# Output projection inside the merges' block, first gather in the cross attention, value weights inside paged attention

## The chip, the cores and the metric

The kernel runs on one core of a Trainium2 chip. The metric is the device time of one execution in microseconds (us); of several executions the median is given. TensorE is PE in the rows (PEld is its weight load), VectorE is DVE, ScalarE ACT, GpSimd POOL, and SP the engine that issues most transfers (SPq its queue).

## The reference, cut to what matters

One layer of a decoder for 1024 prompt tokens and 64 new tokens (8 requests of 8). All branches read the same normalised input `h`.

```
z = h @ w_in, cut into queries, latents, gates, values ...
o_a: prompt: causal attention; new tokens: attention over 4096 cached
     positions per request, whose latent and rotary rows lie in pages
     (cache_kv_latent[page_table], cache_k_rope[page_table])
o_b: gated linear recurrence; its values are one block of 512 columns of z
o_c: attention into 256 memory tokens (memory keys and values per request)
proj = einsum('btne,ned->btnd', [o_a*silu, o_b*silu, o_c*silu], w_branch)
gate = sigmoid(g_raw)                      # three gates of 1024 channels
y = einsum('btd,de->bte', sum_n(gate * proj), w_out)
out = rmsnorm(x + y) * g_final
```

## The kernel before, in words

The program is a row of blocks. In a block each engine has a stream of its own, and the streams meet by semaphores; between blocks all engines meet. Tokens are 1088 columns (1024 prompt, 64 new); `h` and the merged result lie transposed, as 8 chunks of 128 channels.

Products of the projections are made of **split operands**: x is cut into a high part (a mask that clears the low bits, VectorE, `masked`, L884) and a low part (x less the high part, VectorE or GpSimd), ScalarE copies the high part into the rounded type (CAST), and TensorE adds three products: high by high, low by high, high by low. So each weight is loaded, masked, subtracted and copied before its first product.

The blocks that matter here, in order of time:

- **Cross attention** (block L1043, 683.6 to 762.2 us). SP loads the memory keys and values of four requests first (L1048, L1050), four more later. GpSimd only clears `qx` (L1099). TensorE turns the keys (L1198, waits for each request's keys) between the prompt's scores (L1167), turns (L1175) and products (L1184).
- **Paged attention** (block L1337, to 1025.5 us). The 8 requests go in 4 pairs; a pair has one step with the new tokens and 8 steps with a group of cached rows, so STEPS is 36. A group is four indirect transfers by GpSimd (latent rows L1376, rotary rows L1379, for two requests; 1.18 MB in all) into one of 8 slots; a slot is free when its group has been attended (`s_pv`). GpSimd also makes the pair's operands: a copy of the latent queries `qb` (L1363) and the rotary queries spread over quadrants `qpx` (L1365). In step k TensorE does the scores of k (L1530, L1533 for new tokens, L1542, L1546 for groups), turns the probabilities of k-1 (L1557, L1560), turns the rows of group k+1 (L1514, L1519) and attends k-1 (L1570, L1576). VectorE has the maximum of step k (L1424, L1426 or L1428), evacuates the probabilities (L1483, L1485) and half of the turned rows (L1490), keeps sums and accumulates (L1454). ScalarE has the exponentials (L1400, L1403) and the other half (L1411, L1413). SP loads the mask of the new tokens (L1341) and `w_uv` (L1342), after step 9 spills the gated branches to DRAM (L1344, L1345), brings `h`'s high part back (L1349), and spills the new tokens' branch (L1351) as soon as VectorE has gated it. The block ends when that spill has landed. Then the semaphores are cleared (L1609), with an empty block behind.
- **Value projection** (block L1664, to 1090.3 us). SP loads the value weights in four pieces (L1668), then constants. VectorE masks each piece and subtracts pieces 0 and 2 (L1713), GpSimd 1 and 3 (L1690), ScalarE copies (L1697); TensorE goes chunk by chunk over 8 token tiles in 8 banks (L1745).
- **Recurrence**, which the change leaves as it is.
- **Merges** (block L2414, 1495 to 1913.8 us): 48 items, 24 for each half of the tokens; item k is a channel block and a branch. An item is a gate product (48 matmuls, L2623, except two per half) and a branch product (24, L2648) of 272 columns. Its weights are loaded into one of three slots by SP (L2428, L2429) when `s_bp` says that the slot's last item is projected, masked by VectorE three items ahead (`prepare`, L884), subtracted by GpSimd (L2533), copied by ScalarE (L2572). ScalarE makes the sigmoid (L2584), VectorE the product with it (`consume`, L2499), GpSimd adds to the merged result (L2544).
- **Output projection** (block L2706). `w_out` is 4.2 MB, loaded as four pieces (L2713), split as above (VectorE L884, L2778; GpSimd L2805; ScalarE L2740), 8 chunks of 1024 columns. A tile of 128 tokens has its own split (L2770, L2800, L2736) and 48 matmuls of 512 columns (L2822); nine tiles alternate between two pairs of banks. VectorE adds the residual (L2789), ScalarE sums squares and takes the root, VectorE scales (L2763), SP stores (L2711).

The order within each stream is the order of the program text.

## Time and profile before

| what | us |
|---|---|
| median of 3 executions (lowest, highest) | 2040.85 (2038.68, 2044.95) |
| the profiled execution | 2041.31 |
| its span in the profile | 2039.5 |
| mean granted TensorE clock in it | 0.967 of full |

All times in rows are us from the span's start, of this one execution; 1.8 us of its time lie outside the span. In a timeline row the bracket is the idle time of the engine before the instruction and what ended it. Matmuls overlap, so their durations are longer than their spacing. PEclk is the granted clock as a share of full speed, DMA the mean busy share of 16 DMA engines.

### The profile page before, as it was taken

Reading aid. Unit: us, or ns where it says so; the run is one execution under the profiler, and the core shown is the slowest. Engines: PE = TensorE matmul, PEld = TensorE weight load, DVE = VectorE, ACT = ScalarE, POOL = GpSimd, SP = SyncE. Lnnn points to the kernel's source line nnn. Section 1 sums busy time; section 2 is a strip of 40 time slices with the busy share of each in tenths; the row PEclk is TensorE's granted clock in tenths of the full one; section 3 lists DMA queues with packets and bytes.
Section 4 is the critical chain, followed back from the end, with each engine's and each line's share of the span. In section 5 each row is a group of like instructions: output and inputs, shape, how many; then the busy total and the mean of one; then the engine's idle time right before and its main releaser. Section 6 shows DMA issues by size and latency. Waiting matters only on the chain. (4 is left out here: it accounts for less than half of the span.)

```text
span 2039.5 us, 31621 instructions
## 1 busy us (share of the span) xinstructions
PE 1872.0 (92%) x13519; PEld 1521.7 (75%) x13519; DVE 776.7 (38%) x1495; ACT 596.5 (29%) x1160; POOL 510.5 (25%) x392
## 2 busy tenths in 40 slices
PE   5998889887999878999978999999999999999798
PEld 4643455555999635666657989989889999999676
DVE  4025355556000243444421555465552115111432
ACT  3020333334111332323202343433332223222221
POOL 0000000004221007655006700000015454445320
PEclk8998999988999998999989999999999999999899
DMA  8002000001211317865022822222133334333322
GB/s 280 0 0 71 6 11 6 6 1 60 91 42 42 121 47 230 305 218 175 1 78 69 218 63 51 61 51 51 43 113 83 94 82 131 91 94 81 127 73 83
DMA packets 188519, 175.96 MB, mean 86 GB/s; under 512 B 47676, under 2 KB 155772, under 8 KB 188252
## 3 DMA queue, kind: packets, MB, share of 16 engines
q1 hardware_dynamic: 165228, 120.76, 20.2%
q0 software_dynamic: 20592, 52.63, 8.6%
q8 instruction: 107, 1.75, 0.4%
q10 hardware_dynamic: 2560, 0.56, 0.2%
q14 instruction: 32, 0.26, 0.0%
HBM read 153.73 MB, written 27.47 MB: 89 GB/s over the span
## 5 line engine op out<-in xcount | busy, mean ns | idle before, releaser
L884 DVE TENSOR_SCALAR sb<-sb 128x1024 int32<-128x1024 int32 (+4 forms) x127 | 97.8, 777 | 318.9 <-DMA sb<-in_w_branch 160.2
L2533 POOL TENSOR_TENSOR weights_low<-sb 128x1536 fp32r<-128x1536 f32 x42 | 147.1, 3501 | 183.7 <-DVE sb L884 183.7
L2623 PE MATMUL ps<-h_high_again,weights_high 128*128 128x272 f32 x688 | 142.2, 288 | 2.0 <-ACT weights_high L2572 2.0
L2623 PE MATMUL ps<-h_low,weights_high 128*128 128x272 f32 x688 | 142.3, 288 | 0.0
L2623 PE MATMUL ps<-h_high_again,weights_low 128*128 128x272 f32 x688 | 142.2, 288 | 0.0
L615 POOL TENSOR_TENSOR sb<-sb 32x1088 f32<-32x1088 f32 x8 | 19.9, 2483 | 394.1 <-ACT sb L626 394.1
L2160 PE MATMUL ps<-h_high_again,recurrence_weights_high 128*128 128x384 f32 (+1 forms) x432 | 105.4, 353 | 5.4 <-ACT recurrence_weights_high L1918 4.1
L2623 PEld LDWEIGHTS ps<-h_high_again,weights_high 128*128 128x128 f32 x688 | 108.2, 188 | 2.2 <-ACT weights_high L2572 2.2
L2623 PEld LDWEIGHTS ps<-h_high_again,weights_low 128*128 128x128 f32 x688 | 108.4, 188 | 0.0
L2623 PEld LDWEIGHTS ps<-h_low,weights_high 128*128 128x128 f32 x688 | 108.3, 188 | 0.0
L2572 ACT CAST weights_high<-sb 128x1536 fp32r<-128x1536 f32 (+1 forms) x44 | 64.3, 1461 | 130.6 <-POOL weights_low L2533 127.2
L2160 PE MATMUL ps<-h_high_again,recurrence_weights_low 128*128 128x384 f32 (+1 forms) x432 | 97.0, 334 | 0.0
L2160 PE MATMUL ps<-h_low,recurrence_weights_high 128*128 128x384 f32 (+1 forms) x432 | 96.8, 333 | 0.0
L975 PE MATMUL ps<-h_high,gate_weights_high 128*128 128x384 f32 (+1 forms) x384 | 85.5, 331 | 12.1 <-ACT h_high L950 10.8
L454 PE MATMUL ps<-sb 128*128 128x384 f32 (+3 forms) x288 | 89.8, 475 | 3.2 <-DMA sb<-in_w_in 3.2
L1376 POOL DMA_INDIRECT sb<-in_cache_kv_latent,sb x64 | 60.7, 948 | 119.2 <-issue 93.9
L2499 DVE TENSOR_TENSOR sb<-ps,sb 128x544 f32<-128x544 f32 x48 | 34.8, 724 | 137.1 <-PE ps L2648 132.1
L932 POOL TENSOR_TENSOR gate_weights_low<-sb 128x1024 fp32r<-128x1024 f32 x16 | 42.7, 2669 | 174.0 <-DVE sb L884 174.0
L975 PE MATMUL ps<-h_low,gate_weights_high 128*128 128x384 f32 (+1 forms) x384 | 85.7, 331 | 0.0
L975 PE MATMUL ps<-h_high,gate_weights_low 128*128 128x384 f32 (+1 forms) x384 | 85.0, 330 | 0.0
L2160 PEld LDWEIGHTS ps<-h_high_again,recurrence_weights_high 128*128 128x128 f32 x432 | 71.8, 191 | 16.1 <-issue 6.2
L788 PE MATMUL ps<-sb 96*128 96x512 f32 (+3 forms) x192 | 80.8, 532 | 2.6 <-issue 1.2
(337 smaller groups left out, 4020.3 us busy)
## 6 DMA issues: line engine op xcount, KB each, us to landing
sb<-in_w_in SPq DMA_DIRECT2D x82, 512.0 KB, 4.1
sb<-in_w_branch SPq DMA_DIRECT2D x48, 256.0 KB, 4.5
sb<-in_x_prompt SPq DMA_DIRECT2D x16, 512.0 KB, 6.7
values_by_level<-values POOLq DMA_DIRECT2D x56, 128.0 KB, 3.5
sb<-values_by_level POOLq DMA_DIRECT2D x7, 896.0 KB, 7.5
out<-sb SPq DMA_DIRECT2D x10, 512.0 KB, 2.9
h_high_in_dram<-h_high SPq DMA_DIRECT2D x8, 544.0 KB, 6.8
h_high_again<-h_high_in_dram SPq DMA_DIRECT2D x8, 544.0 KB, 12.8
```

The costliest lines, as they stand in the source:

```text
L454: mm = nc.tensor.matmul(bank(4 * (n % 2) + k, cols, 0, tn, r0), slab[sl][:, c, col:col + cols], hT[:, c, t0:t0 + tn], start=c == 0, stop=c ...
L615: nc.gpsimd.tensor_tensor(rot_a[64:96, :], qT3[n % 4][64:96, :], cosT[64:96, :], ALU.mult)\
L788: mm = nc.tensor.matmul(bank(slot + b, n=cols), q[0:QK, 128 * j:128 * j + 128], k[0:QK, 512 * b:512 * b + cols], start=True, stop=diag >= 512)
L884: return nc.vector.tensor_scalar(high.bitcast(I32), x.bitcast(I32), -4096, None, ALU.bitwise_and)
L932: nc.gpsimd.tensor_tensor(flat(zLowR[n % 3]), flat(zLow[n % 3]), flat(zHigh[n % 3]), ALU.subtract)\
L975: mm = nc.tensor.matmul(bank(4 * (n % 2) + s, n=tn), w[n % 3][:, c, :], x[:, t0:t0 + tn], start=c == 0 and part == 0, stop=c == DC - 1 and ...
L1376: nc.gpsimd.indirect_dma_start(out=lat[slot][:, a, :], out_offset=None, in_=lat_rows, in_offset=bass.IndirectOffsetOnAxis(ap=rows, axis=0) ...
L2160: mm = nc.tensor.matmul(bank(s, n=tn), w[a][:, c, :], x[c][:, t0:t0 + tn], start=c == 0 and term8 == 0, stop=c == DC - 1 and term8 == 2)
L2499: nc.vector.tensor_tensor(two(out), src, two(gate_of(k)), ALU.mult).then_inc(s_bt, 1)
L2533: nc.gpsimd.tensor_tensor(flat(wLowR[slot]), flat(wLow[slot]), flat(wHigh[slot]), ALU.subtract)\
L2572: nc.scalar.copy(flat(wHighR[slot][:, c0:DC + 4]), flat(wHigh[slot][:, c0:DC + 4])).then_inc(s_wh, 1)
L2623: mm = nc.tensor.matmul(bank(4 * (k % 2) + s, n=HS2), w[:, c, :], x[:, t0:t0 + HS2], start=c == 0 and part == 0, stop=c == DC - 1 and part ...
```

## The change

**Memory and gathers.** Paged attention's buffers are placed before the cross attention's block, with six slots for gathered groups instead of eight, in places that the cross attention leaves free. The first group's four gathers are issued by GpSimd in the cross attention, right after `qx` is cleared. The copies `qb` go: TensorE reads the latent queries where they lie (`latent_queries`), and for the new tokens the rotary ones too; the wait for the pair's operands moves from the first scores of a pair to the rotary scores of its groups.

**Value weights.** SP loads the four pieces in paged attention, behind `w_uv`. VectorE splits pieces 0 and 1 ahead of steps 27 and 31, ScalarE copies them a step later; pieces 2 and 3 stay in the value projection's block, all on VectorE. The block's end doesn't wait for the spills any more; the merges' SP stream does, after its first load.

**Output projection.** Its block is gone; its streams follow in the merges' block. `w_out` comes in 16 pieces of 128 x 512 (0.26 MB): 8 from item 28 on, two an item, into memory that the first half's tokens leave free, split one an item in items 28 to 35; 8 when item 46 is projected, split by VectorE four before and four after its last merge product. Merged tile 0 is split in item 27 and 28, tile 1 before the last item's product, tile 2 after the last piece, the others when the tile two before is projected. All splits are VectorE's, GpSimd has none. ScalarE takes the root's table ahead (a root of one word) once the last sigmoid is done. Sums, norm and stores are as before; the products of a chunk go by halves of 512 columns.

```diff
+        work = Arena(base, WORDS)
+        LSLOTS = 6
+        HS = HA * NS
+        G = 8
+        PAIRS = NB // 2
+        STEPS = PAIRS * (G + 1)
...
+        s_il0 = sem("first_value_low_ready")
+        s_ih0 = sem("first_value_split")
+
+        def gather(pool, j):
+            p, g, slot = j // G, j % G, j % LSLOTS
+            for a in range(2):
+                rows = rows_of_page[:, G * (2 * p + a) + g:G * (2 * p + a) + g + 1]
+                pool.indirect_dma_start(out=lat[slot][:, a, :], out_offset=None, in_=lat_rows,
+                                        in_offset=bass.IndirectOffsetOnAxis(ap=rows, axis=0)).then_inc(s_kv[slot], 16)
+                pool.indirect_dma_start(out=rop[slot][:, a, :], out_offset=None, in_=rope_rows,
+                                        in_offset=bass.IndirectOffsetOnAxis(ap=rows, axis=0)).then_inc(s_kv[slot], 16)
...
                 nc.gpsimd.memset(qx, 0.0).then_inc(s_qx0, 1)
+                gather(pool, 0)
...
+        FIRST_SPLITS = [STEPS - 9, STEPS - 5]
...
+                for i in range(4):
+                    sp.dma_start(vslab[:, 2 * i:2 * i + 2, :], w_cols[:, 2 * i:2 * i + 2, C_I:C_I + 512]).then_inc(s_vs[i], 16)
                 sp.wait_ge(s_pv, 9)
                 sp.dma_start(spill[:, 4:8, :], gate[:, 8:12, :]).then_inc(s_spill, 16)
...
-                sp.wait_ge(s_spill, 48)
+                for i in range(4):
+                    sp.wait_ge(s_vs[i], 16)
 
             @block.gpsimd
...
-                gather(0)
                 operands(0)
                 for j in range(1, G * PAIRS):
                     if j % G == 4 and j // G + 1 < PAIRS:
                         operands(j // G + 1)
-                    gather(j)
+                    if j >= LSLOTS:
+                        old = j - LSLOTS
+                        pool.wait_ge(s_pv, (G + 1) * (old // G) + old % G + 2)
+                    gather(pool, j)
...
+                    if k - 1 in FIRST_SPLITS:
+                        i = FIRST_SPLITS.index(k - 1)
+                        act.wait_ge(s_il0, i + 1)
+                        nc.scalar.copy(vHighR[i], vHigh[i]).then_inc(s_ih0, 1)
...
+                    if k in FIRST_SPLITS:
+                        i = FIRST_SPLITS.index(k)
+                        dve.wait_ge(s_vs[i], 16)
+                        v = vslab[:, 2 * i:2 * i + 2, :]
+                        masked(vHigh[i], v).then_inc(s_im0, 1)
+                        dve.wait_ge(s_im0, i + 1)
+                        nc.vector.tensor_tensor(vLowR[i], v, vHigh[i], ALU.subtract).then_inc(s_il0, 1)
...
-                        pe.wait_ge(s_rq, 4 * p + 4)
                         for c in range(2):
                             for a in range(2):
-                                nc.tensor.matmul(bank(out, HS, n=TN, r0=HS * a), qb[p % 2][:, a, c, :], ckvNewT[:, c, :],
+                                nc.tensor.matmul(bank(out, HS, n=TN, r0=HS * a), latent_queries(2 * p + a, c), ckvNewT[:, c, :],
...
-                            nc.tensor.matmul(bank(out, HS, r0=HS * a), qb[p % 2][:, a, c, :], latT[:, a, c, :],
+                            nc.tensor.matmul(bank(out, HS, r0=HS * a), latent_queries(2 * p + a, c), latT[:, a, c, :],
                                              start=c == 0, stop=False, skip_group_check=True)
+                    pe.wait_ge(s_rq, 2 * p + 2)
...
-        nc.clear_and_free_semaphores(sems)
+        nc.clear_and_free_semaphores([s for s in sems if s is not s_spill])
...
-                for i in range(4):
-                    sp.dma_start(vslab[:, 2 * i:2 * i + 2, :], w_cols[:, 2 * i:2 * i + 2, C_I:C_I + 512]).then_inc(s_vs[i], 16)
...
-                for i in range(4):
-                    act.wait_ge(s_il[i % 2], i // 2 + 1)
-                    nc.scalar.copy(vHighR[i], vHigh[:, 2 * i:2 * i + 2, :]).then_inc(s_ih, 1)
+                for i in (2, 3):
+                    act.wait_ge(s_il, i - 1)
+                    nc.scalar.copy(vHighR[i], vHigh[i]).then_inc(s_ih, 1)
...
+                for i in (2, 3):
+                    masked(vHigh[i], vslab[:, 2 * i:2 * i + 2, :]).then_inc(s_im, 1)
+                    dve.wait_ge(s_im, i - 1)
+                    nc.vector.tensor_tensor(vLowR[i], vslab[:, 2 * i:2 * i + 2, :], vHigh[i], ALU.subtract).then_inc(s_il, 1)
...
-                    pe.wait_ge(s_ih, c // 2 + 1)
+                    if c >= 4:
+                        pe.wait_ge(s_ih, c // 2 - 1)
...
+        EARLY = 4
+        early_low = [(2 * c + x) * T for c in range(EARLY) for x in range(2)]
+        early_high = [gate_at + (i if i < 4 else i + 4) * T for i in range(2 * EARLY)]
+        late_low = [chunk_at[0] + D * i for i in range(DC - EARLY)]
+        late_high = [w_high_at[1] + D * i for i in range(3)] + [w_low_at[1]]
...
+        FIRST_PIECE = ITEMS + 4
+
+        def pieces_at(k):
+
+            return [k - FIRST_PIECE] if FIRST_PIECE <= k < FIRST_PIECE + 2 * EARLY * 2 else []
...
                 load(2)
+                sp.wait_ge(s_spill, 48)
...
+                def output_weights(p):
+                    c, x = p // 2, p % 2
+                    sp.dma_start(wo[c][x], w_out[0][128 * c:128 * c + 128, 512 * x:512 * x + 512]).then_inc(s_wo[c][x], 16)
                 for k in range(ITEMS + 4, 2 * ITEMS):
                     load(k)
+                    if k == ITEMS + 4:
+                        sp.wait_ge(s_bp, ITEMS)
+                    for p in range(2 * (k - ITEMS - 4), 2 * (k - ITEMS - 4) + 2):
+                        if p < 2 * EARLY:
+                            output_weights(p)
+                sp.wait_ge(s_bp, 2 * ITEMS - 1)
+                for p in range(2 * EARLY, 2 * DC):
+                    output_weights(p)
...
+                sp.wait_ge(s_bp, 2 * ITEMS)
+                sp.wait_ge(s_bt, 2 * ITEMS)
+                sp.wait_ge(s_ba, 4 * DC)
...
+                def output_weights(p):
+                    c, x = p // 2, p % 2
+                    dve.wait_ge(s_wo[c][x], 16)
+                    masked(woHigh[c][x], wo[c][x]).then_inc(s_om, 1)
+                    dve.wait_ge(s_om, p + 1)
+                    nc.vector.tensor_tensor(woLowR[c][x], wo[c][x], woHigh[c][x], ALU.subtract).then_inc(s_ol2, 1)
+
+                def split_first():
+                    dve.wait_ge(s_bp, ITEMS + 2)
+                    dve.wait_ge(s_ba, 2 * DC)
+                    for i in range(2):
+                        y = yT[:, 4 * i:4 * i + 4, 0:128]
+                        masked(y0High[i], y).then_inc(s_ym, 1)
+                        dve.wait_ge(s_ym, i + 1)
+                        nc.vector.tensor_tensor(y0LowR[i], y, y0High[i], ALU.subtract).then_inc(s_yl, 1)
+
+                def split_y(i):
+
+                    if i == 1:
+                        dve.wait_ge(s_bp, 2 * ITEMS - 1)
+                    elif i == 2:
+                        dve.wait_ge(s_bp, 2 * ITEMS)
+                    else:
+                        dve.wait_ge(s_y, i - 2 + 1)
+                    if i == 4:
+                        dve.wait_ge(s_ba, 4 * DC)
+                    r, n = tile_rows[i], (i - 1) % 2
+                    y = yT[:, :, 128 * i:128 * i + r]
+                    masked(yHigh[n][:, :, 0:r], y).then_inc(s_ym, 1)
+                    dve.wait_ge(s_ym, i + 2)
+                    nc.vector.tensor_tensor(yLowR[n][:, :, 0:r], y, yHigh[n][:, :, 0:r], ALU.subtract).then_inc(s_yl, 1)
...
                 for k in range(ITEMS + 2, 2 * ITEMS):
+                    if k == 2 * ITEMS - 1:
+                        split_y(1)
+                        for p in range(2 * EARLY, 2 * DC - 4):
+                            output_weights(p)
                     consume(k)
                     if k + 3 < 2 * ITEMS:
                         prepare(k + 3)
+                    if k == ITEMS + 3:
+                        split_first()
+                    for p in pieces_at(k):
+                        if p < 2 * EARLY:
+                            output_weights(p)
+                for p in range(2 * DC - 4, 2 * DC):
+                    output_weights(p)
+                split_y(2)
+                dve.wait_ge(s_gf, 16)
+                for i in range(NTT):
+                    if i >= 1 and i + 2 < NTT:
+                        split_y(i + 2)
...
+                    if k == ITEMS + 4:
+                        for i in range(2):
+                            act.wait_ge(s_yl, i + 1)
+                            nc.scalar.copy(y0HighR[i], y0High[i]).then_inc(s_yh, 1)
+                    for p in pieces_at(k - 1):
+                        if p < 2 * EARLY:
+                            output_weights(p)
...
+                act.wait_ge(s_gs, gates_through(2 * ITEMS - 2))
+                nc.scalar.activation(small[:, 40:41], sg[0][:, 0:1], ACT.Sqrt)
+                split_y(1)
+                for p in range(2 * EARLY, 2 * DC):
+                    output_weights(p)
+                split_y(2)
+                for i in range(NTT):
+                    if i >= 1 and i + 2 < NTT:
+                        split_y(i + 2)
...
-
-
-        work = Arena(after_small, y_at)
-        wo_at = work.at
...
+                    if i == 0:
+                        pe.wait_ge(s_yh, 2)
+                        pe.wait_ge(s_gs, gates_through(2 * ITEMS - 2))
+                    else:
+                        pe.wait_ge(s_yh, i + 2)
+                    if i == 1:
+                        pe.wait_ge(s_bt, 2 * ITEMS - 1)
+                        low, high = first_y(c) if i == 0 else (yLowR[(i - 1) % 2][:, c, 0:r], yHighR[(i - 1) % 2][:, c, 0:r])
+                        for x in range(2):
+                            if i == 0:
+                                pe.wait_ge(s_oh, 2 * c + x + 1)
+                            for part, (y, w) in enumerate(((high, woHighR[c][x]), (low, woHighR[c][x]), (high, woLowR[c][x]))):
+                                mm = nc.tensor.matmul(bank(2 * (i % 2) + x, r), y, w, start=c == 0 and part == 0,
+                                                      stop=c == DC - 1 and part == 2)
+                for i in range(NTT):
+                    output(i)
```

## Rows read from the trace of the kernel before

**Rows 1.** The page, first part: busy time of each engine in the whole span.
```profile
PE 1872.0 (92%) x13519; PEld 1521.7 (75%) x13519; DVE 776.7 (38%) x1495; ACT 596.5 (29%) x1160; POOL 510.5 (25%) x392
```
**Rows 2.** Waits of TensorE, 1905 to 2040 us: total, times, longest.
```profile
PE ps L2822 <- ACT output_weights_high L2740: 13.9, 3, 12.1
```
**Rows 3.** Timeline of TensorE, 1910 to 1912 us: start, us, engine, line, operation.
```profile
1911.20 0.41 PE L2648 MATMUL ps<-activations_high,weights_low 128*128 128x272 f32 x2
```
**Rows 4.** The chain of work that ended last, in order of time: start, us, what.
```profile
1914.08 4.85 DMA sb<-in_w_out
...
1941.71 89.56 PE ps L2822 x384
```
**Rows 5.** Timeline of all engines, from paged attention to the value projection.
```profile
1025.52 0.37 SPq L1351 DMA_DIRECT2D spill<-sb  x1
1029.42 1.92 SPq L1668 DMA_DIRECT2D sb<-in_w_in  x4
...
1033.36 0.69 DVE L884 TENSOR_SCALAR sb<-sb 128x1024 int32<-128x1024 int32 x1 [7.87 <-DMA sb<-in_w_in]
1034.09 1.23 DVE L1713 TENSOR_TENSOR value_weights_low<-sb 128x1024 fp32r<-128x1024 f32 x1
...
1036.45 0.80 PE L1745 MATMUL ps<-value_weights_high,h_high_again 128*128 128x512 f32 x1 [11.42 <-ACT value_weights_high L1697]
```
**Rows 6.** Timelines of TensorE and GpSimd, start of paged attention.
```profile
763.57 1.05 POOL L1376 DMA_INDIRECT sb<-in_cache_kv_latent,sb  x1 [78.99 <-issue]
770.13 0.70 PE L1530 MATMUL ps<-sb 128*64 128x64 f32 x8 [9.22 <-POOL sb L1365]
770.24 1.00 POOL L1376 DMA_INDIRECT sb<-in_cache_kv_latent,sb  x1 [0.16 <-issue]
774.05 0.94 POOL L1379 DMA_INDIRECT sb<-in_cache_k_rope,sb  x1 [0.31 <-issue]
779.09 1.91 PE L1514 MATMUL ps<-sb 128*128 128x128 f32 x16
```
**Rows 7.** Stretch table, merges: us, busy PE, PEld, DVE, ACT, POOL, PEclk, DMA, GB/s.
```profile
1700.00:1900.00 200.00, 200.00 (x1602) 200.00 (x1601) 48.32 (x60) 50.63 (x52) 97.29 (x38) 1.00 0.35 95
```
**Rows 8.** Timeline of VectorE in paged attention, a step of new tokens, two others.
```profile
957.17 0.23 DVE L1424 TENSOR_TENSOR sb<-ps,sb 128x64 f32<-128x64 f32 x1
959.06 1.29 DVE L1490 COPY sb<-ps 128x512 f32<-128x512 f32 x2 [0.62 <-PE ps L1514]
...
985.50 0.69 DVE L1428 TENSOR_REDUCE sb<-ps 128x1 f32<-128x512 f32 x1 [2.11 <-PE ps L1546]
992.87 0.69 DVE L1428 TENSOR_REDUCE sb<-ps 128x1 f32<-128x512 f32 x1 [2.11 <-PE ps L1546]
```
**Rows 9.** Timeline of VectorE in the merges: masks and subtractions.
```profile
1704.83 0.44 DVE L884 TENSOR_SCALAR sb<-sb 128x544 int32<-128x544 int32 x1
1705.30 0.72 DVE L2467 TENSOR_TENSOR activations_low<-sb 128x544 fp32r<-128x544 f32 x1
1711.94 1.78 DVE L2467 TENSOR_TENSOR activations_low<-sb 128x544 fp32r<-128x544 f32 x1
1889.58 0.96 DVE L884 TENSOR_SCALAR sb<-sb 128x1536 int32<-128x1536 int32 x1 [4.20 <-DMA sb<-in_w_branch]
```
**Rows 10.** Stretch table by 2 us, around the value projection's start.
```profile
1024.00:1026.00 2.00, 1.03 (x32) 0.89 (x30) 0.42 (x1) 0.00 (x0) 0.00 (x0) 0.79 0.00 0
...
1040.00:1042.00 2.00, 2.00 (x6) 1.60 (x5) 1.76 (x4) 1.05 (x1) 1.14 (x1) 0.50 0.20 56
```
**Rows 11.** The line of the latent gathers (L1376), time from issue to landing.
```profile
DMA to landing us min/median/max: 3.9/4.2/10.0
```
**Rows 12.** Cross attention's start: waits of TensorE, its timeline, the stretch table.
```profile
PE ps L1198 <- DMA sb<-in_cache_mem_k: 2.1, 3, 1.3
...
691.92 0.44 PE L1198 MATMUL ps<-sb 128*128 128x128 f32 x2 [1.31 <-DMA sb<-in_cache_mem_k]
...
690.00:692.00 2.00, 0.48 (x3) 0.28 (x4) 0.50 (x3) 0.83 (x3) 0.00 (x0) 1.00 1.05 391
```

More of the change, by code:

```diff
@@ L977, in _ @@
                     mm.then_inc(s_zc, 1)
+        work = Arena(base, WORDS)
[4 more added lines that the diff above has]
+        STEPS = PAIRS * (G + 1)
+        lat = [work.take(2, 4 * KVL) for _ in range(LSLOTS)]
+        maskNew = work.take(PAIRS, TN)
+        vs_at = work.at
+        vslab = work.take(DC, 512)
+        latT = work.take(2, 2, 512)
+        ropT = work.take(2, 128)
+        prob = [work.take(512) for _ in range(2)]
+        probT5 = [work.take(4, 2 * HS) for _ in range(2)]
@@ new lines, in build @@
+        acc = work.take(KVL)
+        oRow = work.take(KVL)
+        newScore = work.take(TN)
+        ngmax = work.take(STEPS)
+        nmax5 = work.take(STEPS)
+        alpha = work.take(STEPS)
+        gsum = work.take(STEPS)
+        lsum = work.take(STEPS)
+        rinv5 = work.take(PAIRS)
+        work.at = after_attn_in + 8992
+        assert work.at + LSLOTS * 8 * ROPE <= qc_at
+        rop = [work.take(2, 4 * ROPE) for _ in range(LSLOTS)]
+        qpx = [work.take(2, 4, HS) for _ in range(2)]
@@ new lines, in build @@
+        wv_all = work.take(2, HA, VA)
+        aNew = work.take(4, TN)
+        work.at = -(-work.at // 8) * 8
+        vh_at = [work.at, work.at + 1024, vs_at + DC * 512, vs_at + DC * 512 + 1024]
+        vHigh = [Arena(at, WORDS).take(2, 512) for at in vh_at]
+        vLowR = [rounded(f"value_weights_low{i}", vs_at + i * 1024, 2, 512) for i in range(4)]
+        vHighR = [rounded(f"value_weights_high{i}", at, 2, 512) for i, at in enumerate(vh_at)]
+        lat_rows = lat_pool[0].rearrange("n (r f) c -> (n r) (f c)", f=4)
@@ L1290, in build @@
         s_rq = sem("pair_operands_ready")
-        s_kv = [sem(f"group_gathered{i}") for i in range(LSLOTS)]
         s_t = sem("group_bank_turned")
@@ L1331, in build @@
         s_spill = sem("branches_in_dram")
-        aNew = work.take(4, TN)
         s_an = sem("new_attention_gates_kept")
@@ new lines, in build @@
+        res = [Arena(after_small + D * i, WORDS).take(D) for i in range(3)] + [Arena(w_high_at[0] - 512, WORDS).take(D)]
+        sqr = Arena(w_high_at[0] + 512, WORDS).take(D)
+        assert after_small + 3 * D <= w_low_at[1] and w_low_at[1] + D <= w_high_at[0] - 512
+        assert w_high_at[0] + 512 + D <= w_high_at[1]
+        xr = [Arena(chunk_at[17] + D * i, WORDS).take(D) for i in range(2)]
+        gfin = Arena(chunk_at[17] + 2 * D, WORDS).take(D)
+        NTT = TILES + 1
+        x_tiles = [x_prompt[0, 128 * i:128 * i + 128, :] for i in range(TILES)] + [x_sample.rearrange("b t d -> (b t) d")]
```

319 lines of the change are left out of this document (106 added, 213 removed).

## The prediction

> **What bounds the kernel now.** I read the page first: TensorE is busy for 92% of the span [rows 1], so the time is TensorE's work plus the places where it stands still. The waits of TensorE, the chain and the timeline then show three such places, all where one block of the program ends and the next begins. The largest is before the output projection: waits of 13.9 us in three places, the longest of 12.1 us [rows 2]. The chain ends there [rows 4]: it starts with the load of `w_out`, 4.85 us, goes through the split of its columns, and is pure TensorE from 1941.71 to 2031.27. The second is between paged attention and the value projection, 11.42 us [rows 5]; the third at the start of paged attention, 9.22 us [rows 6]. The merges themselves hold no idle time: in 200 us TensorE is busy for 200, VectorE for 48, ScalarE for 51, GpSimd for 97 [rows 7]. So work that moves into the merges is free if it keeps to those gaps, and work that moves into paged attention, whose steps of 7.37 us repeat exactly, is free if it fits VectorE's idle 2.11 us of each [rows 8].
>
> **Part 1, output projection in the merges' block.** Removed: the block change, the wait for `w_out`, its split at the pace of VectorE and GpSimd. The new first product follows the last merge product: that pair starts at 1911.20 [rows 3], two instructions at 0.125 us each, so the projection can start at 1911.45. Its rate at full clock: 384 products in 89.56 us [rows 4], 0.2332 each; all 432 (nine tiles of 48) take 100.8 us, so they end at 2012.2 instead of 2031.27. That is **-19.1**; it holds the gap of 12.1 us, the later waits for weights, and the slow clock of the first products. The last tile's addition, norm and store are unchanged and follow as before.
> What has to be ready: half of `w_out` (eight pieces of 512 columns) is loaded and split during items 28 to 35, one piece an item of 9 us. A piece is a mask and a subtraction on VectorE: 0.44 + 0.72 us at 544 columns, or 1.78 for the subtraction beside GpSimd [rows 9], and one ScalarE copy. VectorE gives the mask of the next weights at 1889.58, about 5 us after the item began, and is idle before it for 4.20 us [rows 9]; a piece put behind that mask ends before the next product of the item or up to 2 us after it, and the product's sum is wanted only an item later. The cover is 9 us an item; were it gone, each piece would cost at most its 2.2 us. The load of the next weights stands ahead of the pieces on SP's queue, so they delay no weights of their own item.
> The other half is released when item 46 is projected (1902.7). Eight loads of 0.26 MB: at 1 MB in 4.85 us from issue [rows 4], all 2.1 MB are there by about 1911. VectorE first splits merged tile 1 (0.69 + 1.23, the 1024-column prices of [rows 5]), then four pieces (4.6 us), the last merge product, then four more: last piece about 1917, ScalarE's copy 1917.7. TensorE wants the ninth piece at 1911.45 + 24 x 0.233 = 1917.0 and the sixteenth at 1921.9. So no wait. Later tiles need a split each 11.2 us, which costs VectorE 2.0 us and GpSimd now nothing. The loads of the residual wait for the last merge sum (about 1914, the old block's end) and are wanted at 1922.6.
>
> **Part 2, value weights loaded and half split in paged attention.** Before, the old block ended when the last spill had landed, the next one issued its loads at 1029.42, VectorE got the first at 1033.36, and TensorE began at 1036.45 [rows 5]. Now the block ends with the issue of that spill (1025.52 + 0.37), since its landing is awaited only in the merges; from the landing (about 1027.5) to the first issue took 1.9 us, the clearing of the semaphores in it, so TensorE starts at about 1027.9: **-8.5**. The two pieces still to split are wanted 22 us later and need 2 x 1.92 us. The slow clock there I leave as it is: the granted clock falls in the stretch 1024 to 1026, before the long wait, and is at 0.50 (the 1.2 GHz level) up to 1042 [rows 10], that is until TensorE had worked for some 6 us.
> The Trainium skill (TensorE: Matmul & The Clock Gate, Part 1: The HAM clock gate) says that the slow level is the idle default and that activity releases it. By that, an idle time of 2.9 us instead of 11.4 might not be enough for a fall, and the sum would be 2.6 us better; the row of the fall speaks against it, as it comes with hardly any idle time.
> Inside paged attention the two splits are put at steps 31 and 27. At 31 the 1.92 us fit the 2.11 us of idle. At 27, a step of new tokens, VectorE has no idle time before the maximum (957.17), and 0.62 us later before its copies of 959.06 [rows 8]; the split pushes maximum, exponentials, ScalarE's first copy and so the transposition of the rope rows: 1.92 less what slack there is, **+1.5** (bounds 0 and 1.9).
>
> **Part 3, first gather in the cross attention.** Now GpSimd issues the first group at 763.57, clears its operands, and issues the second from 770.24 to 774.99 [rows 6]; TensorE starts at 770.13 and turns the second group at 779.09. After the change GpSimd has two short products left and starts the second group at about 763.9, ends at 768.9; landed 3.9 to 4.2 us after issue [rows 11], 773. TensorE starts at once, but its own chain (masks, maximum, evacuations, first scores) reaches the second turn not before 771.5. Beside it SP now loads 2.1 MB of value weights, so I take 773.8 for the turn that was at 779.09: **-5.3**. Bounds: 771.5 (-7.6) and, if every byte SP has queued went first at 391 GB/s [rows 12], 776 (-3).
> At the start of the cross attention the DMA engines are full (share 1.05, 391 GB/s), and TensorE waits for memory keys, 2.1 us in three waits, the last at 691.92 [rows 12]. The gather brings 1.18 MB = 3.0 us of that. If it is served behind the keys it costs 0, if it all comes before the last key, 3.0; its issue (four at 1.25 us) runs beside the keys' loads, so I take **+2.2**.
> The Trainium skill (DMA: Bandwidth & Descriptors, Queues, rings and completion order) says that each engine takes turns between the queues it has work for. By that nearly the whole gather comes before the fourth key, and the sum would be 0.8 worse. No row before has both queues on that place.
> **Six slots.** A slot is held from issue to the attended step: 2.3 steps after its turn (16.9 us) + issue 5.0 + landing. Six steps are 44.2 us, so a landing may take 22 us; the longest is 10.0 [rows 11]. Costs 0. The queries are read where they lie, in strips as long as before: 0; two copies a pair leave GpSimd.
>
> **Sum**: +2.2 - 5.3 + 1.5 - 8.5 - 19.1 = -29.2. The profiled execution took 2041.31 us (span 2039.5); 2012.1, and since it lies 0.5 above the median of the runs, 2040.85, the forecast is **2011.6**.
>
> **Rivals.**
> (a) *Both starts are dearer*: the gather costs 3.0, the second turn comes at 776 (-3), the split at step 27 costs 1.9. Sum -25.7: 2015.1. For it: the full DMA engines in [rows 12]. 0.15.
> (b) *The clock doesn't fall at the value projection*: -2.6 more, 2009.0. Speaks for it the shorter idle time, against it the early fall in [rows 10]. 0.12.
> (c) *The projection isn't fed* (the change doesn't do what it says): the late pieces run after the last merge product and at the slow price, 0.44 + 1.78 us [rows 9]: 8 x 2.22 from 1912.4 gives 1930.2, with the copy 1930.8, where TensorE wants the last at 1921.9. Part 1 gives 8.9 less: 2020.5. Against it: GpSimd has nothing to do then. 0.04.
> (d) *Slower: six slots don't cover the gathers.* A step becomes (16.9 + 5.0 + landing)/6 when the landing passes 22 us. At 32 us it is 9.0, + 1.6 in each of 26 groups = 42: 2053. It eats the whole gain from a landing of 29 us on. Against it the longest of 10.0 [rows 11], for it that spill and reload share the engines in this stage. 0.04.
> The forecast itself gets 0.60; 0.05 is left for what I don't see, of which half on no change or slower.
>
> **How the numbers follow.** A measurement can tell about 0.3% (6 us) from no change. Forecast, (a), (b), (c) are all faster by more. Faster 0.93, same 0.02, slower 0.05. The range: part 2 at 11.1, the start at 7.6, gather and split at 0 give 2003; (a) with a waiting TensorE in the projection (2 us) 2017; 2005 to 2018 leaves out (c), (d) and the joint extremes.
>
> **What would show it.** After: the wait before the first output product under 1 us, its 432 products in about 101 us at clock 1.00; TensorE idle for some 3 us between the last product of paged attention and the value projection, then still 6 us at 0.50; the second group's turn some 11.3 us after the block's start (before 16.6); waits for memory keys near 4.3 us; one step of paged attention 1.5 us longer, all others 7.37. It is wrong if TensorE waits on ScalarE in the output projection, if steps of paged attention wait on the gathers' DMA, or if waits show up in the merges.

## Result, and the profile after

The changed kernel takes **2015.91 us** in the median of 4 runs (2012.08 to 2020.78), the kernel before on the same chip 2042.68 us (median of 4). The ratio is 0.9872, 95% interval 0.9844 to 0.9900: 26.8 us less. The forecast was 2011.6, range 2005 to 2018. A second look at the same kernel beside nine runs of before gave 2015.67 (0.9878, 0.9860 to 0.9897). So the sign holds and the size nearly: of the 29.2 us forecast 2.4 are missing in the first measurement and 4.5 in the second. The profiled execution took 2012.08 us, its span 2010.2. Medians here and below are of executions that agree within 1.5%; one of the twelve of the kernel `own_block` took 3974.11 us, for no reason on record, and is left out.

The waits of TensorE over the span. The columns are: who waited, for whom, us in all, times, the longest. They answer to [rows 2, 5, 6 and 12]:

```profile
PE ps L1250 <- DMA sb<-in_cache_mem_k: 4.4, 3, 3.5
PE ps L1549 <- ACT sb L1434: 4.3, 5, 1.9
```

No row names the output weights any more (before 13.9 us), none the value weights (11.4), none GpSimd's operands (9.2). The memory keys' wait (L1250) has doubled from 2.1 us, and so has the rope rows' wait for ScalarE's copies (L1549; L1519 before, 2.1 us); a new wait of the second group shows in the timeline below.

**The end.** VectorE's last merge sum (L2600), the work behind it, and TensorE's row in the chain that ended last (start, us, count):

```profile
1894.17 2.26 DVE L2631 TENSOR_TENSOR merged_low<-sb 128x1024 fp32r<-128x1024 f32 x1
1901.80 0.72 DVE L2600 TENSOR_TENSOR sb<-ps,sb 128x544 f32<-128x544 f32 x1 [1.11 <-PE ps L2850]
1902.89 1.74 DVE L2606 TENSOR_TENSOR output_weights_low<-sb 128x512 fp32r<-128x512 f32 x1
1907.12 0.69 DVE L2606 TENSOR_TENSOR output_weights_low<-sb 128x512 fp32r<-128x512 f32 x1
1907.85 0.62 ACT L2757 CAST output_weights_high<-sb 128x512 fp32r<-128x512 f32 x1 [0.44 <-DVE output_weights_low L2606]
...
1901.76 100.16 PE ps L2889 x432
```

All 432 output products run in one piece at 0.232 us each. From the last merge sum to the end of the span it was 2039.5 - 1911.65 = 127.85 us before and is 2010.2 - 1901.80 = 108.4 now: **-19.45**. The last weight piece is copied 6.7 us after that sum, about four before the product that wants it: that is the 46th, and 45 x 0.232 = 10.4.

**The value projection's start** (timeline):

```profile
1027.04 0.37 SPq L1385 DMA_DIRECT2D spill<-sb  x1
1029.68 0.76 PE L1755 MATMUL ps<-value_weights_high,h_high_again 128*128 128x512 f32 x1 [3.13 <-PEq L1640]
```

and by stretch (columns: busy us and instructions of PE, PEld, DVE, ACT, POOL, then the granted clock, the DMA engines' share and GB/s):

```profile
1028.00:1030.00 2.00, 0.32 (x1) 0.35 (x2) 0.32 (x1) 0.00 (x0) 0.00 (x0) 0.61 0.27 62
1032.00:1034.00 2.00, 2.00 (x6) 1.60 (x5) 1.80 (x3) 1.19 (x2) 0.00 (x0) 0.50 0.50 17
1036.00:1038.00 2.00, 2.00 (x10) 1.65 (x9) 0.11 (x1) 0.00 (x0) 0.00 (x0) 1.00 0.18 51
```

From the issue of the last spill to the first product it is 2.64 us where it was 1036.45 - 1025.52 = 10.93: **-8.3**. The clock falls all the same and stands at 0.50, the 1.2 GHz level, to about 1035.3.

**The cross attention** (timeline and stretches; these answer to [rows 12]):

```profile
694.05 0.69 PE L1250 MATMUL ps<-sb 128*128 128x128 f32 x2 [3.46 <-DMA sb<-in_cache_mem_k]
694.53 1.06 PE L1219 MATMUL ps<-sb 128*128 128x256 f32 x2
```
```profile
692.00:694.00 2.00, 0.00 (x0) 0.00 (x0) 0.00 (x0) 0.00 (x0) 0.00 (x0) 0.98 1.03 399
694.00:696.00 2.00, 1.95 (x10) 1.33 (x14) 0.37 (x2) 0.59 (x1) 0.00 (x0) 0.50 1.05 381
696.00:698.00 2.00, 2.00 (x15) 1.14 (x15) 0.47 (x3) 1.02 (x4) 0.00 (x0) 0.67 1.09 394
```

The DMA engines are full at 381 to 399 GB/s, the longest wait of the keys is 3.5 us (before 1.3), and behind it the clock is at 0.50: L1219's pair takes 1.06 us. From the block's first scores (L1219, 683.51; before 683.68) to SP's first load of the next block it was 762.44 - 683.68 = 78.8 us and is 765.95 - 683.51 = 82.4: **+3.7**. The longer waits are 2.3 of that; TensorE's busy time between 693.5 and 697.5, most of it at 0.50, would be some 1.5 us shorter at full clock, and the two together account for the growth.

**The start of paged attention** (timeline, the turns of the second and the third group; [rows 6]):

```profile
778.54 3.04 PE L1544 MATMUL ps<-sb 128*128 128x128 f32 x16 [2.41 <-DMA sb<-in_cache_k_rope,sb]
786.09 1.91 PE L1544 MATMUL ps<-sb 128*128 128x128 f32 x16
```
```profile
774.00:776.00 2.00, 2.00 (x19) 1.60 (x15) 0.06 (x1) 0.00 (x0) 1.55 (x2) 0.54 1.04 400
780.00:782.00 2.00, 2.00 (x12) 1.67 (x12) 1.08 (x2) 0.49 (x1) 1.69 (x2) 0.50 1.05 395
```

The second group's turn starts 12.6 us after the block's first load (16.65 before), after a wait of 2.4 us for its gather, and runs mostly at half clock (3.04 us). The engines are full here too, with the value weights that SP loads from 767.91. The second turn ran at full speed before (1.91 us) and doesn't now; the third runs at full speed in both kernels, so I compare there. It comes 20.1 us after the block's start, before 785.66 - 762.44 = 23.2: **-3.1**. From it to the last spill's issue there are 240.95 us, before 239.86: **+1.1**, the half splits.

The changed parts sum to 3.7 - 3.1 + 1.1 - 8.3 - 19.45 = -26.05. The two profiled executions differ by 29.2; the rest, -3.1, lies between the value projection's first product and the last merge sum (875.2 before, 872.1 after), where the change only adds the splits of `w_out`'s first half. That the profiled difference is the forecast's 29.2 to the tenth is therefore luck.

### The profile page after: what moved, and what is told of

Read it like the earlier page. It is cut to its first block and busy times, and to the rows that moved or that the text cites. A ratio compares the mean times of both kernels' runs of the same rounds, so it can differ in the third digit from the quotient of the medians.

```text
span 2010.2 us, 31646 instructions
## 1 busy us (share of the span) xinstructions
PE 1868.8 (93%) x13519; PEld 1519.2 (76%) x13519; DVE 815.3 (41%) x1528; ACT 596.8 (30%) x1170; POOL 474.5 (24%) x369
## 5 line engine op out<-in xcount | busy, mean ns | idle before, releaser
L884 DVE TENSOR_SCALAR sb<-sb 128x1024 int32<-128x1024 int32 (+4 forms) x145 | 103.7, 724 | 337.7 <-DMA sb<-in_w_branch 148.2
L975 PE MATMUL ps<-h_high,gate_weights_high 128*128 128x384 f32 (+1 forms) x384 | 85.5, 331 | 12.1 <-ACT h_high L950 10.8
L975 PE MATMUL ps<-h_low,gate_weights_high 128*128 128x384 f32 (+1 forms) x384 | 85.7, 331 | 0.0
L975 PE MATMUL ps<-h_high,gate_weights_low 128*128 128x384 f32 (+1 forms) x384 | 85.0, 330 | 0.0
L454 PEld LDWEIGHTS ps<-sb 128*128 128x128 f32 (+1 forms) x288 | 51.5, 179 | 41.4 <-issue 11.2
L2713 POOL TENSOR_TENSOR sb<-sb 128x544 f32<-128x544 f32 x32 | 44.4, 1387 | 160.5 <-DVE sb L2600 160.2
```

The costliest lines, as they stand in the source:

```text
L454: mm = nc.tensor.matmul(bank(4 * (n % 2) + k, cols, 0, tn, r0), slab[sl][:, c, col:col + cols], hT[:, c, t0:t0 + tn], start=c == 0, stop=c ...
L884: return nc.vector.tensor_scalar(high.bitcast(I32), x.bitcast(I32), -4096, None, ALU.bitwise_and)
L975: mm = nc.tensor.matmul(bank(4 * (n % 2) + s, n=tn), w[n % 3][:, c, :], x[:, t0:t0 + tn], start=c == 0 and part == 0, stop=c == DC - 1 and ...
L2713: nc.gpsimd.tensor_tensor(y, y, term[:, i - 1, :], ALU.add).then_inc(s_ba, 1)
```

## Experiments

Each has a profile and four or five timed executions (own_block eleven); us is the median. The columns on the right are us of the profiled execution: "keys' wait" is TensorE's for the memory keys, "start" is from SP's first load of the paged block to the third group's turn, "paged" from there to the last spill's issue, "cross" from the first scores of the cross attention to that load, all from the trace.

| kernel | us | ratio (95%) | keys' wait | cross | start | paged |
|---|---|---|---|---|---|---|
| before | 2040.1 to 2040.4 | 1 | 2.1 | 78.8 | 23.2 | 239.9 |
| changed, first look | 2015.91 | 0.9872 (0.9844 to 0.9900) | 4.4 | 82.4 | 20.1 | 241.0 |
| changed, again | 2015.67 | 0.9878 (0.9860 to 0.9897) | 5.2 | 85.4 | 21.1 | 241.0 |
| late_gather | 2009.77 | 0.9847 (0.9825 to 0.9870) | 2.2 | 78.9 | 20.8 | 241.0 |
| late_values | 2009.13 | 0.9848 (0.9825 to 0.9870) | 4.0 | 82.2 | 16.9 | 241.0 |
| both_late | 2005.67 | 0.9824 (0.9803 to 0.9845) | 1.9 | 78.6 | 17.1 | 241.0 |
| splits_plain | 2014.64 | 0.9878 (0.9857 to 0.9898) | 5.0 | 85.3 | 21.0 | 239.8 |
| both_late_plain | 2002.77 | 0.9819 (0.9800 to 0.9838) | 2.1 | 78.8 | 16.4 | 239.8 |
| gather_in_paged | 2014.57 | 0.9873 (0.9855 to 0.9890) | 2.1 | 81.5 | 26.0 | 241.0 |
| own_block | 2033.70 | 0.9972 (0.9960 to 0.9984) | 4.1 | 82.2 | 20.8 | 241.0 |
| slots4 | 2016.13 | 0.9884 (0.9870 to 0.9899) | 4.1 | 82.1 | 20.9 | 242.7 |
| slots3 | 2158.57 | 1.0589 (1.0571 to 1.0608) | 5.1 | 85.4 | 21.0 | 382.7 |

**The changed kernel again**, as the measure for the rest.

> The changed kernel as it is. What the parts touched by the change add up to in the two traces is 26.2 us (start of paged attention +0.4, the step splits +1.1, value projection -8.3, output projection -19.45); the other 3.1 us between the two profiled executions lie in the recurrence, which the change leaves alone. If that part is scatter, this run is 26 +- 2 us faster than the kernel before; if the recurrence gains by the change, 29.

The gain is 24.7 us, as for the case that the other 3.1 us are scatter. The traces decide it: from the value projection's first product to the last merge sum the changed kernel takes 874.1 us here and 872.1 in the first look, and over all twelve profiled executions of this study it is 868.8 to 875.2, though no edit below but own_block's reaches it. The kernel before has 875.2, and so has both_late. So the change gains nothing there that these runs could show.

**The first gather held back** until the memory values of the first four requests have landed:

```
                 nc.gpsimd.memset(qx, 0.0).then_inc(s_qx0, 1)
+                pool.wait_ge(s_mv[3], 16)
                 gather(pool, 0)
```

> The first gather waits until the first four requests' memory values have landed. Theory (its 1.18 MB come between the memory keys): waits for memory keys back from 4.4 to about 2.1 us, no slow clock behind them, the cross attention's block 82.5 -> 79.0 us, the whole 3.5 us faster than the changed kernel. Rival (the block is longer for another reason, such as GpSimd's issuing beside VectorE): it stays at 82.5, the whole at 0.

The keys' wait is back at 2.2 us and the cross attention at 78.9, so the whole growth came from the gather's place beside the keys, and the rival (another reason) falls. The stretch that stood at clock 0.50 in the changed kernel, 694 to 696, and the one before it:

```profile
692.00:694.00 2.00, 1.98 (x19) 1.31 (x12) 0.91 (x5) 1.49 (x5) 0.00 (x0) 1.00 1.06 391
694.00:696.00 2.00, 1.86 (x16) 0.85 (x15) 1.20 (x4) 1.98 (x7) 0.00 (x0) 1.00 0.41 143
```

The same bytes in the same queue, later, cost nothing here: the first group is wanted only some 70 us later.

**The value weights held back** until four steps have been attended:

```
+                sp.wait_ge(s_pv, 4)
                 for i in range(4):
                     sp.dma_start(vslab[:, 2 * i:2 * i + 2, :], ...)
```

> The four loads of the value weights wait until four steps of paged attention are attended. Theory (they stand beside the second group's gather): TensorE's wait for that gather goes from 2.4 us to under 0.5, the third group is turned 17 us after the block's start instead of 20.1, the whole 3 us faster than the changed kernel. Rival (TensorE's own chain and the slow clock set the second turn): the third turn stays at 20 us, the whole within 1 us.

```profile
775.76 1.91 PE L1545 MATMUL ps<-sb 128*128 128x128 f32 x16
782.33 1.91 PE L1545 MATMUL ps<-sb 128*128 128x128 f32 x16
```

(Its lines stand one further down.) The second turn waits for no transfer and starts 10.35 us after the block's start, at full clock; the third comes at 16.9. The loads had cost 3.2 us in the first profile and 4.2 in the second. One stretch at half clock ahead of the second turn is not theirs, it is here too; the one behind it (780 to 782 above, at 0.50) is gone:

```profile
773.00:775.00 2.00, 2.00 (x16) 1.39 (x14) 0.00 (x0) 0.00 (x0) 1.57 (x2) 0.50 0.75 207
780.00:782.00 2.00, 2.00 (x23) 1.25 (x20) 0.05 (x1) 0.00 (x0) 1.69 (x3) 1.00 0.76 180
```

**Both held back.**

> Both of the two. Theory: the gains add, 6.5 us faster than the changed kernel, about 33 us faster than the kernel before. Rival (one shared cause, the clock): no more than the better one of the two.

10.0 us under the changed kernel by the medians, where 6.5 were expected; the trace gives 6.9 for the cross attention and 4.0 for the start against the second look, or 3.9 and 3.0 against the first. The two costs are separate and add up: each wait alone mends its own column of the table and leaves the other. What they are worth is some 7 us by the first look; the second had the longer low-clock stretches of the last section in its cross attention, and an interval of the medians is some 4 us to either side.

**Part 3 undone**: `gather(pool, 0)` taken from the cross attention and put before `operands(0)` in the paged block.

> The changed kernel with part 3 undone: the first group is gathered at the start of paged attention, as before, and no longer in the cross attention; the value weights' loads and all else stay. By the prediction part 3 gives 5.3 - 2.2 = 3.1 us, so this kernel would take 2015.7 + 3.1 = 2018.8. By what the two traces show (cross attention 3.5 us longer, third group's turn 3.1 us earlier after the block's start) part 3 costs 0.4 us: 2015.3. By the run in which only this gather was made to wait for the last memory keys (5.9 us gained) the cross attention gains up to 5.9 us here too and the start loses 3 to 5: 2013 to 2015. My theory now is 2013 to 2016; over 2018 the prediction's account of part 3 was right after all.

```profile
774.26 3.68 PE L1544 MATMUL ps<-sb 128*128 128x128 f32 x16 [10.97 <-DMA sb<-in_cache_k_rope,sb]
```

2014.57: within the expected 2013 to 2016; the 2018.8 of the prediction's account lies above all four executions (the highest is 2015.71). The keys wait 2.1 us again, but TensorE stands for 11 us before the first turn, and the third comes at 26.0 instead of about 21. So the gather's gain of 5 to 6 us at the start is real, and the cross attention takes most of it back: 3.3 to 3.7 us, measured against 78.8. (The cross attention of this execution took 81.5 because it held low-clock stretches in other places, of which below.) That leaves some 2 us for part 3; the medians of this kernel and the changed one, 1.1 us apart the other way with intervals of some 4 us to either side, can't tell that from nothing.

**The half splits at steps 29 and 32**, no steps of new tokens:

```
-        FIRST_SPLITS = [STEPS - 9, STEPS - 5]
+        FIRST_SPLITS = [STEPS - 7, STEPS - 4]
```

> The changed kernel with the two half splits of the value weights at the 29th and the 32nd of the 36 steps (counted from 0) in place of the 27th and the 31st; neither of the new two is a step of new tokens. My theory: the split at step 27 delays that step's maximum by 1.1 to 1.5 us and the steps it now stands in have 2.11 us of idle time on VectorE for its 1.92 us, so the time falls by 1.1 to 1.5 us against the changed kernel (about 2014.4), and no step is longer than the others. Rival: the split at step 27 was hidden behind the evacuations too, and the 1.1 us by which the rest of paged attention grew came from elsewhere (the DMA engines, the clock): then no change, 0 +- 0.5.

The medians, 1.0 apart where an interval is some 4 us to either side, can't tell. The trace can: the seven executions with the splits at 27 and 31 and six slots give 240.95 to 241.03 for the paged stage, the two with 29 and 32 give 239.8, and before had 239.9 without any split. The split at 27 costs 1.1 to 1.2 us, and on the plain steps both are free. In the changed kernel it stands just ahead of the maximum of the new tokens (L1447), as foreseen:

```profile
957.43 0.69 DVE L884 TENSOR_SCALAR sb<-sb 128x1024 int32<-128x1024 int32 x1
958.15 1.23 DVE L1505 TENSOR_TENSOR value_weights_low<-sb 128x1024 fp32r<-128x1024 f32 x1
959.29 0.22 DVE L1447 TENSOR_TENSOR sb<-ps,sb 128x64 f32<-128x64 f32 x1
```

**Part 1 undone**: the output projection as a block of its own, with the old tiles, loads and splits, and the wait for the last spill still in the merges' block.

> The changed kernel with part 1 undone: the output projection is again a block of its own, as before, with its four loads of w_out, the split by VectorE and GpSimd and the wait for them at its start; the other two parts stay. My theory: part 1 is worth 19.1 to 19.5 us whatever the other parts do, so this kernel takes 2015 + 19 = about 2035 us, the wait of TensorE ahead of its first product is again about 12 us and the chain again starts with the load of w_out. Rival: part of the 19.4 between the two traces is that the merges ran differently, or the clock of the last stage: then under 17 us, and a difference in the merges themselves would show between the value projection and the last merge product.

The waits of its TensorE behind the merges, and two rows of its chain:

```profile
PE ps L2834 <- ACT output_weights_high L2752: 15.3, 3, 12.9
PE ps L2834 <- ACT merged_high L2748: 1.5, 1, 1.5
```
```profile
1902.19 5.68 DMA sb<-in_w_out
...
1930.66 89.56 PE ps L2834 x384
```

18.0 us above the changed kernel's second look and 17.8 above its first, where the traces give 19.45 and, from this kernel's last merge sum at 1899.76 to its end at 2028.4, 128.6 - 108.4 = 20.2. Part 1 is worth 18 to 20 us on its own; the rival (part of it elsewhere, under 17 us) falls.

**Three slots, then four**, with the memory of six left as it is (`LSLOTS = 3`, `LSLOTS = 4`).

> The changed kernel with three gather slots in place of six (the memory of the other three stays unused). Theory, by the formula of rival (d): a slot is held for 2.3 steps after its turn, 16.9 us, plus issue 5.0 and landing 4.2, 26.1 us for three groups, so a group can come every 8.7 us and no faster, where a step takes 7.37. If every group pays it, that is 1.3 us x 29 groups = 38 us; but the four steps of new tokens use no slot, so that a group is wanted only every 7.37 x 9/8 = 8.3 us on average, and the least is 0.4 us x 29 = 12 us. Expected: 12 to 38 us above the changed kernel, with waits of TensorE on the gathers' DMA. Rival: a slot is released earlier than I hold, under 22.1 us a round, and the time stays within 1 us of the changed kernel.

It was 143 us, not 12 to 38: a miss, and of the formula itself. The wait of the turns over paged attention, and three turns in the middle of it:

```profile
PE ps L1544 <- DMA sb<-in_cache_k_rope,sb: 105.7, 26, 9.4
```
```profile
918.83 3.68 PE L1544 MATMUL ps<-sb 128*128 128x128 f32 x16 [4.21 <-DMA sb<-in_cache_k_rope,sb]
932.73 3.68 PE L1544 MATMUL ps<-sb 128*128 128x128 f32 x16 [4.25 <-DMA sb<-in_cache_k_rope,sb]
946.57 3.68 PE L1544 MATMUL ps<-sb 128*128 128x128 f32 x16 [4.31 <-DMA sb<-in_cache_k_rope,sb]
```

A step takes 13.9 us. I had held the 2.3 steps between a turn and the last use of its group at 16.9 us; but they are steps of whatever length a step has. With step P and n slots, n P = 2.3 P + issue + landing, so P = (issue + landing)/(n - 2.3) = 9.2/0.7 = 13.1 us. Each wait also brings the low clock: the turns take 3.68 us and not 1.91.

The timeline of the same steps, TensorE and GpSimd, corrects both constants:

```profile
922.86 2.45 PE L1606 MATMUL ps<-sb 128*64 128x256 f32 x16
925.59 0.94 POOL L1030 DMA_INDIRECT sb<-in_cache_kv_latent,sb  x1 [9.14 <-PE ps L1606]
```

A group is turned, and two steps later attended (L1606), right after the turn of that step. The hold is thus 2P and the 6.5 us from 918.83 to 925.3, and from there to the turn of the group that takes the slot, at 932.73, it is 7.4 us. So 3P = 2P + 6.5 + 7.4, P = 13.9, as measured. At full clock the 6.5 us are 4.4 (884.69 to 889.05 in the changed kernel): a hold of 2.6 steps, not 2.3.

> The changed kernel with four gather slots in place of six (the memory of the other two stays unused). The run with three slots (143 us above the changed kernel, where I had 12 to 38) corrects my formula: the 2.3 steps from a group's turn to its last use are counted in steps of the new length, so n slots give a step of (issue + landing)/(n - 2.3), which for three slots is 9.2/0.7 = 13 us. For four it is 9.2/1.7 = 5.4 us, less than the 7.37 a step takes, and a gather waits only where its landing passes 1.7 x 7.37 - 5.0 = 7.5 us, which the longest of the changed kernel does by 0.2. Expected: the time of the changed kernel, 2015 to 2016, or up to 5 us more where the value weights' loads make a landing longer. Rival: the formula of rival (d) as written, which holds the slot for a fixed 26.1 us: 6.5 us a step, no cost either, so this run cannot tell the two apart below the bound, but if the held time is in truth 38 us (three slots, read by that formula: 12.8 us x 3) four slots give 9.6 us a step and 40 us or more above the changed kernel.

2016.13, no difference from the changed kernel: 9.2/1.7 = 5.4 us, or (4.4 + 7.4)/2 = 5.9 by the corrected constants, is less than a step. The rival's 40 us did not come. The waits for gathers grew from one of 2.4 or 3.5 us to three of 4.8 us together:

```profile
PE ps L1544 <- DMA sb<-in_cache_k_rope,sb: 4.8, 3, 2.8
```

and the paged stage by 1.7 us, so four slots stand at the edge and six have room. The rule itself rests on the three-slot kernel, from which it was made; that four cost next to nothing agrees with it, but agrees with the fixed hold of rival (d) too.

**All three corrections together** (the two waits, and the splits at 29 and 32):

> Three edits to the changed kernel together: GpSimd waits for the last memory keys before it issues the first gather, SP waits for the fourth attended step before it loads the value weights, and the half splits stand at steps 29 and 32. My theory: the first two together gave 10.0 us against the changed kernel, the third gives its 1.1 to 1.5 us independently: about 2004.4, the lowest time so far. Rival: the split at step 27 costs nothing on the clock of this kernel: 2005.7, as without the third edit.

2002.77 us, ratio 0.9819: the best kernel of this study, 37 us under before and 13 under the changed one. Part of its interval overlaps that of both_late, so the third edit rests on the paged stage's 239.8 against 241.0, not on the medians.

## Why the prediction was right, and where it was off

- **Part 1, -19.1**: right; 19.45 in the traces, 18.0 by undoing it. The cover held as argued: no wait in the merges and none in 432 products. Tile 1's subtraction took 2.26 us beside GpSimd, not 1.23, and one piece 1.74, not 0.69; the loads came early enough that it ended 6.7 us after the last sum where I had some 6. Rival (c), the unfed projection, is out.
- **Part 2, -8.5**: -8.3. No run undoes this part alone, but in all eleven profiles of kernels that have it the first product comes 2.63 to 2.65 us after that spill's issue. The clock fell though the idle time was 3.1 us and not 11.4, as I took from the row of the fall in [rows 10]; rival (b) is out. So the 2.6 us by which the rule of the Trainium skill (TensorE: Matmul & The Clock Gate, Part 1: The HAM clock gate) could have made the sum better did not come. **Split at step 27, +1.5**: 1.1 to 1.2, inside its bounds.
- **Part 3's start, -5.3**: the term that was mis-sized. Without the loads the mechanism gives what I took and more: late_values has the second turn at 10.35 us (I had 11.3 with the loads, and 9.1 for the bare chain, in which no stretch at half clock stood) and the third 6.3 us earlier than before. With them the third turn comes only 3.1 us earlier in the first profile and 2.1 in the second. The step that failed is "Beside it SP now loads 2.1 MB of value weights, so I take 773.8". It had two faults: the chain under it was 1.3 us longer than my 9.1, loads or not, and the turn was late by the gather's wait *and* then ran at half clock, for which I had no term. I had put the loads at 2.3 us over the chain's 771.5; that is right for the second turn in the first profile (2.2; 3.2 in the second), but at the third turn they cost 3.2 to 4.2.
- **The memory keys, +2.2**: the wait grew by 2.3 us, to the predicted place (4.4 us for "near 4.3"), but the block grew by 3.7 (3.3 to 3.7 in the four executions without a late low-clock stretch), outside the bound of 3.0. Again the missing term is the clock: 694 to 698 ran at 0.50 and 0.67. In the first look the last of the three key waits took nearly all the growth, from 1.3 to 3.5 us; in the second it shared it with the one before it (1.8 and 2.9). Over the seven executions with the gather beside the keys the waits' sum is 4.0 to 5.2 us, 1.9 to 3.1 above before. What I had worked out from the rule of the Trainium skill by which an engine takes turns between its queues (DMA: Bandwidth & Descriptors, Queues, rings and completion order) was 3.0, the top of what was seen; my 2.2 is in its lower half.
- **Six slots, 0**: right, four would do. But the hold is 4.4 us and two steps, 19.1 us and not 16.9, and rival (d) was priced by a formula in which it is fixed: its threshold is near the right one and its slope too flat. A landing of 32 us would, by an estimate from the three-slot rows, have made the step some 10 us and not 9.0.
- **The total.** Rival (a), both starts dearer, was nearer than the forecast: the two starts and the split gave 3.7 - 3.1 + 1.1 = +1.7 where the forecast had -1.6 and (a) +1.9. That is 3.3 us; with 0.2 that the value projection took and 0.35 that part 1 gave back, the parts gained 3.1 us less than the 29.2 forecast. The medians say 2.4 and 4.5 less, which agrees. The time itself came out 4.3 over the forecast also because the kernel before measured 2042.68 beside it and not 2040.85.
- **Waits the prediction passed over.** It names three places where TensorE stands still. The same list of waits has sums as long elsewhere (L803 24.9 us, L288 18.0, L975 10.8), which the change leaves as they are.

## What to carry to other kernels

A load moved into another stage is free only if nothing there waits for the same DMA engines at that moment: here the same two sets of transfers, each held back by one wait until the burst beside it was over, gave some 7 us more than the change had by the traces, 10 by the medians. Price a wait of TensorE by its length plus what the products behind it lose at the low clock; here some 2 us more of it cost 3.3 to 3.7. And for a ring of n buffers count the hold in steps of the new length: n P = held steps x P + refill, so that three buffers in place of six cost 143 us where a hold fixed in us had promised 12 to 38.

## What the runs showed that I had not expected

The same program does not have its low-clock stretches in the same places. The last stretches of the cross attention in the second look at the changed kernel, 756 to 760 and 760 to 764:

```profile
756.00:760.00 4.00, 1.78 (x11) 1.04 (x10) 2.68 (x11) 2.19 (x8) 0.00 (x0) 0.97 0.00 0
760.00:764.00 4.00, 3.69 (x6) 1.70 (x7) 0.00 (x0) 0.16 (x1) 0.00 (x0) 0.60 0.00 0
```

In the first look the same work, after the same short waits, runs at full clock:

```profile
756.00:760.00 4.00, 2.03 (x14) 1.19 (x12) 3.11 (x13) 2.03 (x7) 0.00 (x0) 1.00 0.00 0
760.00:764.00 4.00, 3.45 (x10) 1.44 (x8) 0.00 (x0) 0.37 (x1) 0.00 (x0) 1.00 0.00 0
```

The eight products (L1236) that end the block, and the wait before them, first look and second:

```profile
760.75 3.67 PE L1236 MATMUL ps<-sb 128*128 128x512 f32 x8 [0.55 <-ACT sb L1118]
760.31 5.10 PE L1236 MATMUL ps<-sb 128*128 128x512 f32 x8 [0.55 <-ACT sb L1118]
```

That is 1.4 of the 3.0 us between the two cross attentions (85.4 and 82.4). The keys' waits are 0.8 of it, and the rest goes with a stretch at 0.50 behind the keys that lasted some 6 us and not 4. Four of the twelve executions profiled (again, splits_plain, slots3, gather_in_paged, the ones with 85.4, 85.3 and 81.5) have it, at 0.57 to 0.69 over 4 us, the others have not. Between the value projection and the merges, too, the kernel before had such a stretch where the changed kernel had none, which, by its length and its clock, is about 1.7 us of the 3.1 between the two:

```profile
1404.00:1408.00 4.00, 4.00 (x16) 3.85 (x15) 1.65 (x5) 2.12 (x3) 0.00 (x0) 0.57 0.00 0
```

What starts these stretches is left open; no run here was made to find it. A single profile of this kernel is therefore good to some 6 us (the stretch between value projection and last merge sum ranges over 6.4), while a stage without such a stretch repeats to 0.1 us (240.95 to 241.03 in seven executions), and that is what settled the split's 1.1 us, which the medians could not.
